# Expert stage of a two-block model: order of SP's loads, of Pool's row gathers and of DVE's side dots

## What is computed

```python
expert = i1[top_c // 16] * 128 + i2[top_c % 16]      # 8 heads x 16 of 16384 experts for each token
gate = softmax(top_s)
act = gelu(einsum("pd,ped->pe", xb, take(u, eb)))    # u, v: 16384 x 1024, float32
out = einsum("pe,ped->pd", gb * act, take(v, eb))
```

## Time and profile before

| | us |
|---|---|
| median of 3 runs | 5345.15 |
| lowest, highest | 5344.71, 5349.12 |
| span of the profiled execution | 5338.9 |
| expert stage within it | about 1422 to 2517 |

### The profile page before, as it was taken

One profiled execution on the slowest core, in us unless ns is written; L12 is line 12 of the kernel. 1 busy time (PEld: TensorE's weight loads), 2 busy tenths in 40 slices (PEclk: granted clock), 3 DMA queues, 4 the chain that ended last, 5 costly groups with the idle time before them and its releaser, 6 DMA issues.

```text
span 5338.9 us, 67117 instructions
## 1 busy us (share of the span) xinstructions
PE 4931.0 (92%) x27321; PEld 4145.3 (78%) x27321; DVE 3090.8 (58%) x5380; ACT 1910.7 (36%) x2848; POOL 1212.2 (23%) x1009
## 2 busy tenths in 40 slices
PE   7998999998899999989899999999999899889999
PEld 7887878787688878878668777778888677667787
DVE  4544456689657777776542534456666544454555
ACT  3445422235732222223342424322322443343332
POOL 1111000047644555543120002100000120021000
PEclk8999999999999999999899999999999999999999
DMA  4111124422568888875101011122322101112222
GB/s 155 49 52 57 40 80 141 158 89 111 213 247 295 306 304 307 318 283 192 52 14 68 24 40 34 44 95 101 113 103 103 50 28 65 37 52 95 87 92 74
DMA packets 157154, 636.29 MB, mean 119 GB/s; under 512 B 12352, under 2 KB 62544, under 8 KB 106288
## 3 DMA queue, kind: packets, MB, share of 16 engines
q1 hardware_dynamic: 112528, 467.97, 24.3%
q0 software_dynamic: 42240, 160.88, 8.4%
q10 hardware_dynamic: 2080, 3.15, 0.2%
HBM read 595.25 MB, written 36.70 MB: 118 GB/s over the span
## 4 chain that ended last, share of the span: by engine, by line
PE 64%; DVE 15%; ACT 7%; POOL 6%; issue 4%; DMA 4%; SPq 0%; DVEq 0%; ACTq 0%; POOLq 0%
PE banks L269 51%; ACT high L203 2%; DVE low L218 2%; PE banks L2958 2%; POOL ownv L2339 2%; PE banks L2963 2%; DVE ownu L2349 1%; DVE cols L2989 1%; POOL ge L2490 1%; PE banks L3057 1%; DVE oa L2275 1%; ACT P L3007 1%; PE banks L3084 1%; DMA raw<-uT_in 1%; PE banks L1022 1%
## 5 line engine op out<-in xcount | busy, mean ns | idle before, releaser
L218 DVE TENSOR_TENSOR low<-raw,high 128x2048 fp32r<-128x2048 f32 (+2 forms) x333 | 730.3, 2194 | 797.7 <-ACT high L203 775.3
L269 PE MATMUL banks<-UH,high 128*128 128x512 f32 (+2 forms) x2784 | 1016.9, 365 | 44.8 <-DVE UL L510 12.5
L269 PE MATMUL banks<-UL,high 128*128 128x512 f32 (+2 forms) x2784 | 1004.0, 361 | 0.0
L269 PE MATMUL banks<-UH,low 128*128 128x512 f32 (+2 forms) x2784 | 1002.8, 360 | 0.0
L203 ACT ACTIVATE high<-raw 128x2048 fp32r<-128x2048 f32 (+3 forms) x341 | 617.3, 1816 | 762.1 <-DMA raw<-uT_in 272.6
L269 PEld LDWEIGHTS banks<-UH,high 128*128 128x128 f32 (+1 forms) x2784 | 526.3, 189 | 146.3 <-issue 40.6
L269 PEld LDWEIGHTS banks<-UH,low 128*128 128x128 f32 (+1 forms) x2784 | 526.8, 189 | 86.3
L269 PEld LDWEIGHTS banks<-UL,high 128*128 128x128 f32 (+1 forms) x2784 | 526.6, 189 | 82.8 <-issue 0.7
L269 PE MATMUL banks<-UpH,high 128*128 128x384 f32 (+1 forms) x1152 | 404.7, 351 | 58.0 <-issue 29.5
L269 PE MATMUL banks<-UpH,low 128*128 128x384 f32 (+1 forms) x1152 | 400.7, 348 | 0.0
L269 PE MATMUL banks<-UpL,high 128*128 128x384 f32 (+1 forms) x1152 | 400.5, 348 | 0.0
(11 more groups left out here) (423 smaller groups left out, 9981.4 us busy)
## 6 DMA issues: line engine op xcount, KB each, us to landing
raw<-uT_in SPq DMA_DIRECT2D x64, 1024.0 KB
raw<-ev_in SPq DMA_DIRECT2D x64, 1024.0 KB
raw<-up_in SPq DMA_DIRECT2D x44, 1024.0 KB
raw<-ada_in SPq DMA_DIRECT2D x40, 1024.0 KB
gd<-stage SPq DMA_DIRECT2D x12, 2048.0 KB, 6.6
gt<-gd SPq DMA_DIRECT2D x32, 768.0 KB, 5.8
side<-ada_in SPq DMA_DIRECT2D x24, 1024.0 KB, 5.0
raw<-gate_in SPq DMA_DIRECT2D x24, 1024.0 KB
```

The source lines that it names most:

```text
L218: v.e.tensor_tensor(k.low[j % RAW][:, 0:w], k.raw[j % RAW][:, 0:w], k.high[i % SPL][:, 0:w].bitcast(F32), ALU.subtract).then_inc(*v.inc("w ...
L269: ins = pe.e.matmul(out, x, y, start=start and i == 0 and j == 0, stop=stop and i == n - 1 and j == 2)
```

## The change

Three orders change; no instruction is added or taken away.

- **SP**: in a round, the raw loads of u and v come first. The side load and the gates load of round n-1 are issued behind the raw loads of round n, with the waits that they had.
- **Pool**: the weighing becomes a function of its own, `weigh_pool`. A round is now: weigh half 0, u gathers, weigh half 1, v gathers. The first fill of the u buffers (round 7) and of the v buffers (round 13) stays ahead of weigh half 0.
- **DVE**: `dots_dve` takes a range of column halves. A side round now does one half of the side dots ahead of `actL` of half 0 and one half behind it.

```diff
-def dots_dve(k, S, tile, n, t, MOD, key):
+def dots_dve(k, S, tile, n, t, MOD, key, cs=range(2)):
...
-    for c in range(2):
+    for c in cs:
...
+def weigh_pool(k, n, i):
+    g = k.pool
+    j = n // 2
+    s3 = k.ge[i][:].rearrange("p (n t) -> p n t", t=BT)
+    g.wait_ge(f"gates_in{j % 2}", j)
+    g.wait_ge("gelu", (n, i))
+    g.e.tensor_tensor(s3, s3, k.gt[j % 2][:, :, (n % 2) * 2 + i, :], ALU.mult).then_inc(*g.inc("weighed", (n, i)))
+
+
 def experts_pool(k):
...
     for n in range(NT):
-        for s in dots_at(n - 1):
-            if s + NUB < NSLOT:
-                own_row_pool(k, "u", s + NUB)
...
+        weigh_pool(k, n, 0)
+        for s in dots_at(n - 1):
+            if s + NUB < NSLOT:
+                own_row_pool(k, "u", s + NUB)
+        weigh_pool(k, n, 1)
         for s in sums_at(n - 1):
             if s + NVB < NSLOT:
                 own_row_pool(k, "v", s + NVB)
-        j = n // 2
-        g.wait_ge(f"gates_in{j % 2}", j)
-        for i in range(2):
-            s3 = k.ge[i][:].rearrange("p (n t) -> p n t", t=BT)
-            g.wait_ge("gelu", (n, i))
-            g.e.tensor_tensor(s3, s3, k.gt[j % 2][:, :, (n % 2) * 2 + i, :], ALU.mult).then_inc(*g.inc("weighed", (n, i)))
...
                 v.wait_ge(f"side_in{t % 2}", t)
-                dots_dve(k, k.dots3, k.side[t % 2], t, t, k.MOD[1], ("side", t))
+                dots_dve(k, k.dots3, k.side[t % 2], t, t, k.MOD[1], ("side", t), range(0, 1))
+            low(0)
+            if t is not None:
+                dots_dve(k, k.dots3, k.side[t % 2], t, t, k.MOD[1], ("side", t), range(1, 2))
                 if t == NSIDE - 1:
                     bias_dve(k, k.MOD[1], vec(k, "b_ada0"), 0, 48, ("side", t), ("side", 0))
-            low(0)
...
     for n in range(NT + 1):
-        if n < NT:
-            if n >= NE:
-                turn_sp(k)
-            if side_at(n) is not None:
-                load_side(k, side_at(n) + 2)
-            if n % 2 == 1 and n // 2 + 2 < NT // 2:
-                load_gates(k, n // 2 + 2)
+        if NE <= n < NT:
+            turn_sp(k)
         if n:
             turn_sp(k)
+            m = n - 1
+            if side_at(m) is not None:
+                load_side(k, side_at(m) + 2)
+            if m % 2 == 1 and m // 2 + 2 < NT // 2:
+                load_gates(k, m // 2 + 2)
```

## The result

The changed kernel takes 5249.74 us (median of 4, 5244.54 to 5252.27) against 5347.09 us of the kernel before in the same comparison: a ratio of 0.982, 95% interval 0.9808 to 0.9831. The forecast was 5268, its range 5254 to 5312.

A forecast was written before the change was run, and what follows sets the result against it. PE, the busiest engine, idles in the expert stage while own rows move, held by two loops. 49.86 rounds at 17.14 us give 855 instead of 932.5: 5338.9 - 77.5 = 5261.4, plus 6.2 for the median: 5268 us, range 5254 to 5312.

The forecast's parts named there:

- the pace of PE in the sum: Expert stage: 49.86 rounds on PE at 17.14 us make 855 us instead of 932.5, so 77.5 us gone.
- The other two terms: Rest of the kernel left unchanged in the 5338.9 us execution; median of the runs put 6.2 us above that execution.
- Own rows, side and gates leave some unevenness: PE in the expert rounds: the reason given for taking 17.14 us a round and not 16.95.
- Loop one: DVE's own dots, Pool's row gathers, both weighings, next own dots: 18.8 us for a round with three slots.
- new loop one: First own dot, u gathers, weigh 1, act's high and low halves, next dot: about 7.9 us, no longer binding.
- Loop two: Through SP: waits for side dots or second weighing hold back raw u; ACT waits 190.9 us for it.
- SP's and DVE's moved steps at no cost: Later side and gates loads on SP cost nothing, hidden behind over a PE round each; DVE's bursts are covered too.
- the cover of 8 us: DVE's low of the next u tile ends by 25.6 us in the round count; PE needs it at 34.
- The v gathers behind weigh 1: Pool issues v gathers later in a round; DVE's sums were to have no wait at the median landing of 6.3 us.
- The slower rival: DVE's sums wait for v rows, delaying low of the next u: 5386 us at a 21 us mean landing; chance 0.06.
- The transfers as a rival: DMA transfers become the bound in the expert rounds, capped near 322 GB/s: 5296 us, or 5285 to 5330; chance 0.20.
- The port rule: Pool's weighings exclude DVE work: DVE's round 17.2 us, sum 3 us longer, 5271; no chance of its own given.

## Why the prediction was right or wrong

**What bounds the kernel: right.** The loss was PE's idle time from 1585 on, and all of it is gone.

**The step that failed is the pace of PE in the sum.** The prediction had the ceiling at 87 us and took 77.5, from 16.95 us a round ("the best pace of the chain") and 17.14 ("held over seven rounds"). The measured round is 16.70. It stood in the trace of before. First the two matmuls at the start and the two at the end of the 16.95 us piece, then the starts of the u tiles in two successive rounds, before the change and after it:

```profile
1585.16 0.47 PE L269 MATMUL banks<-high,actH 128*128 128x512 f32 x1
1585.47 0.39 PE L269 MATMUL banks<-low,actH 128*128 128x512 f32 x1
...
1601.60 0.34 PE L269 MATMUL banks<-UpL,high 128*128 128x384 f32 x1
1601.77 0.34 PE L269 MATMUL banks<-UpH,low 128*128 128x384 f32 x1
...
2458.93 0.34 PE L269 MATMUL banks<-UpH,high 128*128 128x384 f32 x1
...
2475.64 0.34 PE L269 MATMUL banks<-UpH,high 128*128 128x384 f32 x1
...
1912.31 0.34 PE L269 MATMUL banks<-UpH,high 128*128 128x384 f32 x1
...
1929.01 0.34 PE L269 MATMUL banks<-UpH,high 128*128 128x384 f32 x1
```

2475.64 - 2458.93 = 16.71 before, 1929.01 - 1912.31 = 16.70 after. A piece of the chain runs from the start of its first matmul to the end of its last. The rows overlap: one of 0.34 us is followed by the next start after 0.17. So the piece of 16.95 us holds 0.17 us at its end that a following round would not pay again. At its start, where PE had come late to the tile, the second matmul follows after 0.31 us instead of 0.23. 16.70 + 0.17 + 0.08 = 16.95.

The piece of 127.34 us begins behind a stall, with a granted clock of 0.83 in its first 10 us. It is not seven rounds and 0.43 but seven rounds of 16.70 and one v tile of 8.4, 125.3 us. Of the 2.0 us more, 1.6 are eleven matmuls from 2391.42 on that follow each other about every 0.32 us instead of 0.17; the rest lies at its two ends and at one late tile. Dividing matmuls by 84 was a second slip of the same term, of 2 us in the other direction: the 72 that are left over 49 rounds are two v tiles, matmuls of 512 columns.

With the measured pace the work left at 1585.16 was 49 rounds of 16.70 and two v tiles of 8.4, about 835 us, so 97 us were to be had and not 87. The stage gave 95.55 of them: at its start PE's matmuls kept the slow pace until 1439.0 after the change and only until 1435.9 before, which is 1.5 us. So the value taken was too low by 18 us, and the range, whose lower end was that ceiling less 4, could not hold the result. The other two terms cancel by luck: the rest of the kernel took 4.0 us more, and the median stood 2.3 us above the profiled span, not 6.2. 5267.6 - 18.0 + 4.0 - 3.9 = 5249.7.

**"Own rows, side and gates leave some unevenness": wrong.** None of it reached PE (700.00 of 700). Without own rows the stage is 1.3 us shorter, and without the split of the side dots it is as long.

**Loop one: right**, in its size too. Left alone it gives 5312.9 and 5310.7 where the expectation from its 18.8 us had 5316. The terms of the new loop one add up to 8.0 us and not 7.9, which changes nothing.

**Loop two: right in place, incomplete in what it is.** The prediction saw SP's wait for the side dots and the raw load behind it. It took the gates load for an equal partner; the runs show that the side load alone carries it (5314.66 with it alone against 5312.9, and with Pool's new order 5249.02). It gave the loop no length. The expectation for Pool's order alone did (31 us for two rounds) and left out the gathers, low v, the own dots and sums and low u, which the chain with the side load ahead of raw u holds in its 38.97 us.

**The parts do not add.** SP's order alone gives 29 us, Pool's costs 100, both together give 98. The prediction said nothing of this, since it worked out each part with the other in place; the expectation for Pool's order alone, made from the same numbers, was off by 150 us. The part on Pool overlooked one thing: under SP's old order weigh 1 and DVE's queue release SP's loads, and gathers between the weighings, which now start behind gelu 0, are then in series with raw u's landing. That the side load's place closes this chain is shown by the two runs that move one load each; how the 100 us divide between the series and the longer landings is open.

**SP's and DVE's moved steps at no cost: right.** The gates now take 12.9 us to land at the median instead of 6.5, and nobody waits for them. Without the split of the side dots nothing changes, as the cover of 8 us said.

**The v gathers behind weigh 1: right.** DVE waited 4.3 us for them in 700. The slower rival's price was not tested cleanly.

**The transfers as a rival: too likely.** 0.20 went to a cap of about 322 GB/s, taken from the best 50 us. The kernel after moves 341 over 700 us, and with more copies 403. The rate of a stretch in which the engines are idle 15% of the time is a demand, not a cap; the 412 GB/s over 10 us was the row that told the limit.

**The port rule.** The Trainium skill, "SBUF — State Buffer", section "Who interferes with whom", has two-input DVE instructions and GpSimd instructions that read SBUF exclude each other. The trace agrees. This low half runs on DVE while the weighing at 1905.49, shown above with its 2.25 us, begins:

```profile
1904.58 2.28 DVE L218 TENSOR_TENSOR low<-raw,high 128x2048 fp32r<-128x2048 f32 x1
```

It ends at 1906.86 and the weighing at 1907.74, 0.88 us later. From 1600 to 2300 after the change 12 weighings begin during a low half, and each ends 0.87 or 0.88 us behind it. Weighings got longer, 1403 to 1505 ns on the mean, with DVE busier (0.90 against 0.77 of the time). At this size it moved nothing: Pool has 6 us of a round to spare and PE lost none of the 700 us. The 3 us that this rival would have added did not come.

## What to carry over

Take the pace of the bounding engine from the distance between starts of the same tile in two undisturbed rounds, not from the length of a merged piece, and let the range reach beyond the ceiling that follows. On an in-order queue, a load whose buffer is free can stand behind a load that waits for another engine; it then waits for everything in that engine's queue. Put the loads that the bounding engine needs first, and those that are used rounds later behind them. Two reorderings that each look right can need each other; cost each one also with the other absent.

## What the runs showed of the hardware

- With one core at work the DMA engines moved 403 GB/s over 500 us (share 1.02), of which 346 had been there without the DRAM to DRAM copies, and PE lost under 1% of its time to it. At 341 GB/s (0.91) ACT waited 12.1 us of 700 for raw tiles and DVE 4.3 for v rows.
- How long a 1 MB load took differed by what was issued beside it. A raw u that ACT waited for took 7.4 us at the median in the kernel before, where in the round of the earlier trace rows the first gather began 5 us behind the load, 11.0 with Pool's order alone, where v gathers were issued at the same moment as the loads (2007.98 and 2008.27), and 10.0 with the v gathers ahead of weigh 1. The rate over all was lower in the second (271 against 303 GB/s). No run changed this alone.
- A Pool instruction that began during a low half on DVE ended a fixed time behind it, from 1600 to 2300 after the change: 12 weighings by 0.87 to 0.88 us, and 47 row gathers by 0.81 to 0.86 us. A gather took 1.85 to 3.03 us then, and 0.94 at the least otherwise.
- PE at 16.70 us a round kept a granted clock of 1.00, the level of 2.4 GHz, from 1440 us to the end of the stage. With Pool's order alone, where PE stood idle for 94 of 700 us, it read 0.93, and 0.99 in the kernel before with 57 us idle. PE's busy time per matmul was then 215.7 ns (605.64 us for 2808), 205.3 before and 198.9 after. What that added to the 100 us was not separated.
